# Where pairs of light expert units stand in the order of work of a two-layer decoder trunk

## The reference

```
def swiglu(x, w1, w3, w2):
    return (jax.nn.silu(x @ w1) * (x @ w3)) @ w2

def moe(hn, w_router, w1, w3, w2):
    logits = (t @ w_router).astype(jnp.float32)
    top_v, top_i = lax.top_k(logits, TOP_K)          # TOP_K = 2
    top_w = jax.nn.softmax(top_v, axis=-1)
    combine = jnp.sum(jax.nn.one_hot(top_i, N_EXPERTS) * top_w[..., None], axis=1)
    for e in range(N_EXPERTS):
        out = out + combine[:, e:e + 1] * swiglu(t, w1[e], w3[e], w2[e])
```

## Time and profile before

| what | us |
|---|---|
| median of three runs | 1246.42 (1245.04 to 1246.46) |
| the profiled execution | 1245.6 |
| its span | 1244.0 |
| TensorE busy | 1220.0 (98%) |
| VectorE busy | 815.6 (66%) |
| ScalarE busy | 662.8 (53%) |
| DMA, mean over the span | 315 GB/s, 391.90 MB |

### The profile page before, as it was taken

One profiled execution on the slowest core, in us unless ns is written; L12 is line 12 of the kernel. 1 busy time (PEld: TensorE's weight loads), 2 busy tenths in 40 slices (PEclk: granted clock), 3 DMA queues, 4 the chain that ended last, 5 costly groups with the idle time before them and its releaser, 6 DMA issues.

```text
span 1244.0 us, 15719 instructions
## 1 busy us (share of the span) xinstructions
PE 1220.0 (98%) x6167; PEld 932.6 (75%) x6167; DVE 815.6 (66%) x783; ACT 662.8 (53%) x683; POOL 86.8 (7%) x77
## 2 busy tenths in 40 slices
PE   9999999999999999999999999999999999999988
PEld 7778888888888888887776756677765667765776
DVE  6867766566455766769667566556765567656687
ACT  7577445444336576367564445454464545544664
POOL 0600002000002501010000000000000000000110
PEclk9999999999999999999999999999999999999999
DMA  9753449555545443459999999999999999999993
GB/s 380 286 203 135 170 170 338 223 191 178 203 148 215 167 177 140 171 210 372 421 421 420 421 421 406 421 420 421 420 421 421 423 414 421 421 421 421 422 416 128
DMA packets 56686, 391.90 MB, mean 315 GB/s; under 512 B 6720, under 2 KB 6720, under 8 KB 11584
## 3 DMA queue, kind: packets, MB, share of 16 engines
q1 hardware_dynamic: 53104, 374.84, 75.4%
q0 software_dynamic: 3360, 15.74, 3.4%
q10 hardware_dynamic: 144, 0.26, 0.1%
HBM read 384.78 MB, written 11.80 MB: 319 GB/s over the span
## 4 chain that ended last, share of the span: by engine, by line
PE 75%; DMA 12%; DVE 5%; issue 4%; ACT 2%; POOL 1%; SPq 1%; DVEq 0%; ACTq 0%; POOLq 0%
PE ps L579 20%; PE ps L581 20%; PE ps L580 19%; DMA raw<-in_units 11%; PE ps L1709 10%; PE ps L1251 3%; DVE wl L574 3%; ACT wh L544 2%; DMA h<-in_x 1%; POOL rst L712 1%; PE ps L1310 1%; DVE h L2331 0%; PE ps L1578 0%; PE ps L1629 0%; DVE mix L2049 0%
## 5 line engine op out<-in xcount | busy, mean ns | idle before, releaser
L574 DVE TENSOR_TENSOR wl<-raw,wh 128x2048 fp32r<-128x2048 f32 x250 | 575.0, 2302 | 324.9 <-ACT wh L544 324.0
L544 ACT ACTIVATE wh<-raw 128x2048 fp32r<-128x2048 f32 x250 | 479.2, 1918 | 359.6 <-DMA raw<-in_units 197.4
L579 PE MATMUL ps<-wh,XT_h 128*128 128x512 f32 x944 | 376.2, 399 | 1.3 <-DVE wl L574 1.1
L581 PE MATMUL ps<-wh,XT_l 128*128 128x512 f32 x944 | 368.3, 390 | 0.0
L580 PE MATMUL ps<-wl,XT_h 128*128 128x512 f32 x944 | 367.7, 390 | 0.0
L579 PEld LDWEIGHTS ps<-wh,XT_h 128*128 128x128 f32 x944 | 177.3, 188 | 52.8 <-issue 15.0
L581 PEld LDWEIGHTS ps<-wh,XT_l 128*128 128x128 f32 x944 | 177.1, 188 | 37.9
L580 PEld LDWEIGHTS ps<-wl,XT_h 128*128 128x128 f32 x944 | 177.5, 188 | 34.3
L1709 PE MATMUL ps<-raw,few_X 128*64 128x256 f32 x1056 | 124.6, 384 | 8.3 <-DMA raw<-in_units 8.2
L1709 PEld LDWEIGHTS ps<-raw,few_X 128*64 128x64 f32 x1056 | 73.0, 136 | 55.2 <-issue 18.4
L579 PE MATMUL ps<-wh,moe_gT_h 128*128 128x512 f32 x220 | 89.0, 405 | 1.4 <-DVE wl L562 0.7
(11 more groups left out here) (288 smaller groups left out, 986.1 us busy)
## 6 DMA issues: line engine op xcount, KB each, us to landing
raw<-in_units SPq DMA_DIRECT2D x350, 1024.0 KB, 10.5
x_rows<-in_zeros POOLq DMA_DIRECT2D x8, 512.0 KB, 8.9
raw<-in_boot SPq DMA_DIRECT2D x5, 512.0 KB, 7.4
back<-x_rows POOLq DMA_DIRECT2D x4, 512.0 KB, 8.1
y_rows<-xs POOLq DMA_DIRECT2D x4, 512.0 KB, 8.5
y_rows<-in_zeros POOLq DMA_DIRECT2D x6, 256.0 KB, 17.0
h<-in_x SPq DMA_DIRECT2D x1, 1024.0 KB, 12.9
rows<-in_rows SPq DMA_DIRECT2D x1, 896.0 KB, 17.2
```

What stands on the lines that cost most here:

```text
L544: nc.scalar.activation(wh[:, U.split_slot(j), :], raw[:, U.raw_slot(j), :], ACT.Copy).then_inc(hi_ready, 1)
L574: nc.vector.tensor_tensor(wl[:, s, :], raw[:, U.raw_slot(j), :], wh[:, s, :].bitcast(F32), ALU.subtract).then_inc(lo_ready, 1)
L579: nc.tensor.matmul(o, xh, bh, start=start, stop=False)
L581: return nc.tensor.matmul(o, xl, bh, start=False, stop=stop)
```

## The change

In `moe_orders`, a pair (or the single) goes to the end of the list of use, as it goes to the end of the list of loads. `IN_USE` becomes equal to `LOADED`: each light unit comes two heavy units later than before, on all four engines that follow the list. The order of the loads stays.

```
@@ -87,7 +87,7 @@
         while due - done >= 2 or done < due == len(few):
             two = few[done:done + 2]
             loaded += two
-            used[-2:-2] = two
+            used += two
             done += len(two)
     return loaded, used
```

## The result

The changed kernel takes 1285.3 us (median of 4 runs, 1282.4 to 1286.8) against 1246.0 for the kernel before beside it: ratio 1.031, 95% interval 1.029 to 1.033, 39.3 us slower. I forecast 1254.0, in a range that ended at 1264. The sign and the kind of mechanism were right, the size was a fifth of what came.

What follows compares the result with a forecast made beforehand. The expert stage was taken to run at the pace of its weight loads, 2.49 us per unit at 421 GB/s. Dry DMA time + 9.5 and tail - 1.9 gave + 7.6 us, 1254.0 us, range 1245 to 1264.

Steps and rivals of the forecast that it cites:

- step 3: Ten light pairs of experts 2 and 6: TensorE's wait for the light product holds later slots over the limit, 4.0 us.
- step 4: End of the gate phase, light unit 22: transposes between the pair's units wait; 4.8 us (experts 2, 6), 0.7 (expert 4).
- step 1: Light slots: holdable 9.8 us if loads are issued 4.8 us ahead; two heavy units more fit, so free.
- step 6: Tail after the last light unit: result gathers fall on loads with more cover, 1.9 us gained (bounds 0 and 3.2).
- rival C: Faster: TensorE's waits for light landings were the real cost; half of 19.3 us and the tail won, 1235; chance 0.06.
- n: Number of the heavy unit loaded just before a light pair.
- T: Landing time of the second light unit of a pair.
- Step 2: VectorE's light product falls behind a later heavy unit's split; TensorE's next heavy unit starts 9.95 us after the pair's landing.
- Step 5: Sum on the DMA: 9.5 us with nothing queued, which nothing gives back.
- A: No measurable change: the light slots come back in time and only the tail counts, 1244.5; chance 0.17.
- B: Clearly slower: a short load queue is slower everywhere, at each of 33 pairs of experts 2 and 6; about 1267; chance 0.14.

Runs made afterwards that it cites:

- the two caps: Kernel before, the queue issuing a load only when the one two (three) places before it has landed: 1312.8 us with two, 1248.6 with three.
- the one on the clock: Changed kernel with 8 (narrow slice: 4) small matmuls on TensorE ahead of its wait for the light product, experts 2 and 6: 1284.7 us.

## Why the prediction was wrong

Taken off one after the other, in the only order that was tried, the parts of the loss are (each give or take some 4 us):

| part | predicted | measured | from |
|---|---|---|---|
| product behind the split (step 3) | 4.0 | 12.1 | 1285.3 - 1273.2 |
| light narrow slices (step 4) | 5.5 | 15.0 | 1273.2 - 1258.3 |
| heavy narrow slice | not seen | 5.2 | 1258.3 - 1253.0 |
| what is left, the longer hold above all (step 1) | 0 | 5.8 | 1253.0 - 1247.3 |
| tail (step 6) | -1.9 | in the rows above | gaps 3.2 to 1.3 us |

The rows add up to 38.1, not 39.3, since the kernel before ran at 1246.0 beside the first kernel and at 1247.3 beside the last. And a row is what one more step of hoisting gave back, not what its place costs in the changed kernel: the waits at the narrow slices grew when those of step 3 were gone.

**What bounds the kernel** was right: all of the loss stands in the landings, and the share of TensorE's busy time (98% to 96%) hardly tells of it. One number was read wrongly. The 19.3 us of waits for light landings add PE's and PEld's rows, which tell of the same stall; at 684.56 in the trace of before both have it, 1.45 and 1.90 us. The 11.3 us of PE's row alone are TensorE's. It bore on rival C alone.

**Step 1 failed.** It priced the longer hold by itself at nothing. Held 7.9 us with the order of the kernel before, the slots cost 8.0 us; held 7.4 us in the moved order with the waits gone, up to 5.8. The wrong term is the lead. I took the 4.7 to 4.9 us of a load alone as the lead that a load needs. Two under way gave every load just that at best and lost 0.28 us a load; three gave 7.3 us and lost nearly nothing. With 7.3 in place of 4.8 the limit of step 1 would be 14.94 - 7.3 - 0.34 = 7.3 us, which is its lowest value, not its measure. Single units place it more nearly. In ten traces (the changed kernel's and those of all experiments but the two caps and the one on the clock), the load into a light unit's slot lands late against that unit's own landing + 14.94 us by 0.3 us in the mean where the slot was held under 6 us (220 units, median 0), 0.5 at 7 to 8 us (249), 1.1 at 8 to 9 (166), 2.4 at 9 to 10 (56), 2.3 at 10 to 11 (53), 3.3 at 12 to 13 (27); my formula gives 0 up to 10 us, then 0.4 and 2.4. So the cost begins at some 8 us from landing to the next issue, not at 10.1. The whole kernels agree in order: 5.3 us held cost 1.4 us (within the noise), 7.4 us 5.8, 7.9 us 8.0, 10.4 us 63. Why a load that is issued 5 to 7 us ahead comes late stays open.

The Trainium skill (DMA: Bandwidth & Descriptors, Anatomy of one DMA) would have led further off: its 4.4 us for a load of this size gives a limit of 10.2 us and gave 1250.0. It states its fit for one DMA that GpSimd issues; the loads here are SP's, and one alone took 4.7 to 4.9 us. The runs show that neither is the number that a queue needs.

**Step 2 was right** in mechanism and time: ten waits of TensorE (26.2 us), and in the pair shown heavy unit n + 1 starts at 1046.64, T + 9.8, where I had T + 9.95.

**Step 3** was mis-sized: 12.1 us came back when its waits were taken off, not 4.0. Most of it is the hold and not the limit. The first light unit behind each of the ten waits was to be held 9.9 to 10.5 us from its landing to the end of its matmuls. It was 11.4 in the mean, 9.3 to 13.0. My own limit of 9.8 makes 16.7 us over the ten out of these holds; the loads into the ten slots came 23.7 us late in all. So the larger part was lost by holds that I had too short, the rest by the limit of step 1 (and some 3 us of it come late where nothing is held long, too). Behind the pair shown above, the unit landed at 1046.75 and its matmuls ended at 1056.62 + 1.80 = 1058.42: 11.7 us, by my limit 1.9 too long, and the two loads behind came 4.00 and 2.96 us after the ones before them, 1.98 us over the cadence. There it was the clock. The granted clock (third from the end) falls behind the stall:

```profile
1046.60:1050.20 3.60, 3.60 (x11) 2.86 (x11) 3.18 (x3) 0.10 (x1) 0.00 (x0) 0.56 0.99 416
```

Matmuls of one kind start every 1.28 us instead of 0.69 for some 3 us, and the three heavy units up to the next pair take 1056.62 - 1046.64 = 9.98 us where I had 8.31. What part of the 12.1 the clock has stays open; the run that kept the clock up did not get it back.

**Step 4** was right as to place, and in the changed kernel as to time: the second down unit of experts 2 and 6 is done at T + 12.8 and T + 12.3, where I had T + 12.3, and the load into its slot comes 3.0 and 2.4 us late, where I had 2.5. The 15.0 us of the table are of another kernel, the one without the waits of step 3. There TensorE stands for 5.3 and 6.2 us, has a granted clock of 0.50 and 0.54 behind it, takes 3.41 us for the eight light matmuls instead of the 1.94 of the earlier trace rows, and is done at T + 14.4 and T + 14.0. **And step 4 missed the mirror case.** I asked whom the move of the light work puts behind a split, and not who else stands behind a split that is now reached late: heavy expert 0's narrow slice. Before, the light pair was used ahead of the two heavy units, and that split was not on TensorE's path; now TensorE comes to unit 22 with nothing else to do while the load of unit 23 has the pair ahead of it. In the changed kernel the earlier waits hide it (0.7 us); with them gone it is 5.8 us of stall, and worth 5.2 us (with expert 4's narrow slice, which was hoisted in the same run; they were not told apart).

**Step 5** called it dry time that nothing gives back. That held: 40.4 us more slip in the landings, 39.3 us in the time.

**Step 6** was right in the rows. After the gathers of the kernel after (1226.6 to 1234.4) the landings are stretched as before (timeline, ScalarE):

```profile
1237.86 1.92 ACT L544 ACTIVATE wh<-raw 128x2048 fp32r<-128x2048 f32 x1 [1.00 <-DMA raw<-in_units]
1241.62 1.92 ACT L544 ACTIVATE wh<-raw 128x2048 fp32r<-128x2048 f32 x1 [1.84 <-DMA raw<-in_units]
```

But TensorE is covered (table by stretches):

```profile
1226.00:1240.00 14.00, 14.00 (x65) 11.57 (x65) 13.43 (x10) 10.56 (x7) 9.72 (x4) 1.00 1.01 416
1240.00:1252.00 12.00, 10.74 (x51) 8.62 (x50) 9.89 (x8) 7.71 (x7) 0.00 (x0) 1.00 1.02 422
```

TensorE's gaps there are 0.0 and 1.3 us, against 0.9 and 2.3 in the earlier trace rows. Whether those 1.9 us reach the end of the kernel was not tested by itself.

**The rivals.** A rested on "slots back in time" and fell with step 1. B, a short queue that is slower everywhere, came nearest in size (1267) and is right in part: a thin queue costs before it is dry, and the loss in expert 4's stretch that I named as its sign is there, if small (415 GB/s from 800 to 950 us, 421 before; 3.1 us by the run that moved expert 4 alone). But its picture of each of 33 pairs losing alike is wrong, since with the waits gone the same pairs hold 7.4 us and lose 5.8 us in all. C fell: no run moved more than 420 GB/s from 600 to 1180 us. Of the signs I named, the median from issue to landing fell only to 9.7 where I had 7 or 8 (the lowest did fall to 4.7): the queue is full between the pairs and thin for a few loads behind each. The median hid what the lowest values showed.

## What to carry to other kernels

Before a buffer is held longer, measure the lead that a load needs with others under way, by capping the number of loads in flight, not from the latency of a load alone: here one load alone took 4.8 us, but the stream lost 66 us with that lead and 2 us with 7.3. When a stall is priced, add what comes behind it: here the holds after it were 11.4 us, not 10.1. And when one wait is taken away, look at what it had hidden: the stalls at the narrow slices grew from about 1 us to 5 or 6. When work is moved in a list that several in-order engines follow, look on every engine at what it then stands behind, above all a look-ahead that waits for a load issued after the moved work, and do so for the work that stays as well as for what moves. A product of 0.4 us that was taken ahead of such a wait gave back 12 us.

## What the runs showed that I had not expected

- A load of 1 MiB takes 4.8 us alone; with one other under way 5.1 in the median, but 5.5 in the mean, and from 4.8 on; 7.3 with two others, nearly the 7.5 that three loads take at 2.49 us each. Two under way moved 377 GB/s from 600 to 1180 us, three 418, the kernel before 420.
- A load issued 3 to 4 us before the landing of the one ahead came 1.0 us late in the mean in the changed kernel (15 of them), where the queue had just been dry or nearly so, and 0.3 late in the run with two under way (25). The lead alone does not set it. Loads that SP issues close together after a long wait may share the engines and all land late; that is only argued.
- After TensorE stood for 3.02 us behind a light pair, the granted clock was 0.56 from 1046.6 to 1050.2 us, the 1.2 GHz level and the way back to 2.4, for some 3 us of the next heavy unit. It made the next light unit's hold 1.6 us longer than I had it, but its price could not be told from nothing in the time of the kernel.
